# A third of the modulation's weighted sums moved from the Vector engine to GpSimd

## The reference, cut to what matters

```
def ada_modulation(cond, w, b):
    m = jax.nn.silu(cond) @ w + b
    return jnp.split(m[:, None, :], 6, axis=-1)

m_lat = ada_modulation(c, ada_w, ada_b)          # six rows of 2048
m_ctx = ada_modulation(c_ctx[None, :], ada_w, ada_b)   # rows 0 and 1 are used
hl = modulate(rmsnorm(x_lat, norm_mix), m_lat[0], m_lat[1])
x_lat = x_lat + m_lat[2] * (y_l @ w_out)
hf = modulate(rmsnorm(x_lat, norm_ffn), m_lat[3], m_lat[4])
x_lat = x_lat + m_lat[5] * peer_ffn(hf, ...)
```

## Time and profile before

| what | value |
| --- | --- |
| three runs, median | 3455.74 us (3451.08 to 3463.58) |
| profiled execution, its own time | 3448.01 us |
| its span | 3446.2 us |
| PE busy | 3109.8 us (90%) |
| DVE busy | 2464.3 us (72%) |
| ACT busy | 1886.5 us (55%) |
| POOL busy | 315.6 us (9%) |
| DVE's weighted sums, L573 | 128 instructions, 301.0 us |

### The profile page before, as it was taken

The page is one execution under the profiler, slowest core; times in us unless marked ns, Lnnn a source line. Parts: engine busy times, 40 slices in busy tenths (PEclk is TensorE's granted clock), DMA queues, the critical chain, the costliest instruction groups (busy, mean ns, idle before and its releaser), DMA issues. The chain is left out here.

```text
span 3446.2 us, 45071 instructions
## 1 busy us (share of the span) xinstructions
PE 3109.8 (90%) x12410; PEld 2161.8 (63%) x12410; DVE 2464.3 (72%) x4379; ACT 1886.5 (55%) x4137; POOL 315.6 (9%) x422
## 2 busy tenths in 40 slices
PE   5999988999999999967778489999999899999996
PEld 4887766887887878755556322222222588888885
DVE  5778766887767568753775889988888655555555
ACT  4555544555546655432344277787777555555553
POOL 0000000000000000000000033333333100000000
PEclk9999998999999999967888755555555799999998
DMA  5666664766766558930444199999999755555553
GB/s 194 211 212 220 190 200 160 256 232 228 236 219 221 173 153 275 346 141 7 154 163 167 43 374 381 366 366 386 383 383 380 269 194 187 192 195 187 191 195 122
DMA packets 213971, 788.41 MB, mean 229 GB/s; under 512 B 18515, under 2 KB 19667, under 8 KB 151251
## 3 DMA queue, kind: packets, MB, share of 16 engines
q1 hardware_dynamic: 159904, 407.33, 35.3%
q0 software_dynamic: 50688, 369.12, 28.6%
q10 hardware_dynamic: 3252, 10.41, 0.8%
HBM read 781.55 MB, written 5.24 MB: 228 GB/s over the span
## 5 line engine op out<-in xcount | busy, mean ns | idle before, releaser
L520 ACT ACTIVATE w_hi<-raw 128x512 fp32r<-128x512 f32 x880 | 545.6, 631 | 654.2 <-PE bank L535 596.4
L524 DVE TENSOR_TENSOR w_lo<-raw,w_hi 128x512 fp32r<-128x512 f32 x944 | 626.0, 693 | 350.8 <-ACT w_hi L520 333.8
L2182 DVE CUSTOM_DVE_ANT_0 u_ring<-u_ring,bank 128x1024 f32<-128x1024 f32 x512 | 604.6, 1218 | 79.1 <-DMA u_ring<-in_peer_u,idx 65.3
L533 PE MATMUL bank<-w_hi,xt_hi 128*128 128x512 f32 x1376 | 556.8, 405 | 28.5 <-DVE w_lo L524 28.3
L2249 DVE TENSOR_TENSOR w_lo<-v_raw,w_hi 128x512 fp32r<-128x512 f32 x512 | 354.4, 693 | 298.8 <-ACT w_hi L2233 298.8
L2094 PE MATMUL bank<-row_ring,three 3*128 3x512 bf16 x1024 | 517.3, 616 | 35.7 <-DVE act_in L2182 18.4
L535 PE MATMUL bank<-w_hi,xt_lo 128*128 128x512 f32 x1376 | 540.2, 393 | 0.0
L534 PE MATMUL bank<-w_lo,xt_hi 128*128 128x512 f32 x1376 | 540.1, 392 | 0.0
L2233 ACT ACTIVATE w_hi<-v_raw 128x512 fp32r<-128x512 f32 x512 | 323.8, 633 | 331.4 <-PE bank L2271 327.2
L2269 PE MATMUL bank<-w_hi,vw_hi 128*128 128x512 f32 x1024 | 404.3, 395 | 7.1 <-DVE w_lo L2249 7.1
L2271 PE MATMUL bank<-w_hi,vw_lo 128*128 128x512 f32 x1024 | 401.9, 393 | 0.0
(11 more groups left out here) (405 smaller groups left out, 3865.6 us busy)
## 6 DMA issues: line engine op xcount, KB each, us to landing
v_raw<-in_peer_v SPq DMA_DIRECT2D x128, 1024.0 KB, 4.8
ada_ring<-in_ada_w POOLq DMA_DIRECT2D x96, 1024.0 KB, 5.9
raw<-in_w_in_ab SPq DMA_DIRECT2D x128, 512.0 KB, 3.9
raw<-in_w_in_c SPq DMA_DIRECT2D x128, 512.0 KB, 4.4
raw<-in_w_in SPq DMA_DIRECT2D x120, 512.0 KB, 4.5
raw<-in_w_out_ab SPq DMA_DIRECT2D x32, 512.0 KB, 4.7
raw<-in_w_out_c SPq DMA_DIRECT2D x32, 512.0 KB, 5.7
raw<-in_w_out SPq DMA_DIRECT2D x32, 512.0 KB, 6.5
```

What stands on the lines that cost most here:

```text
L520: act.activation(w_hi[:, s % WS, :], raw[:, q % RAW, s % KC, :], ACT.Copy).then_inc(hi_ready, 1)
L524: dve.tensor_tensor(w_lo[:, s % WS, :], raw[:, s // KC % RAW, s % KC, :], w_hi[:, s % WS, :].bitcast(F32), ALU.subtract).then_inc(raw_used, 1)
L533: pe.matmul(o, a_hi, b_hi, start=kk == 0, stop=False, skip_group_check=True)
L2182: dve.tensor_tensor_reduce(u, u, bank[:, 2 * hf:2 * hf + 2, :].rearrange("p b n -> p (b n)"), 1.0, 0.0, ALU.mult, ALU.add, (act_in, act_ha ...
```

## The change

GpSimd forms the sums of the first 8 blocks of group 2, the first 8 of group 3 and all 16 of group 5. For each block it issues the load of the next one, waits for its own, multiplies the block by the factor in place (`tensor_scalar`), drains, and adds it to `acc` (`tensor_tensor`). The first block of group 3 is multiplied straight into `acc[0]`. DVE keeps the other 96 instructions. In the latent GEMM the 24 that are left there stand 13/3 steps apart, where 28 stood 11/3 apart. The memset of `acc[0]` at s == 17 of the GEMM out of c goes. The semaphore `row_summed` is replaced by a wait for `ada_used`.

```diff
+            pool.wait_ge(rows_cleared, 1)
             for k in range(K):
                 load(k, 0, k)
                 if k % 4 == 3:
                     weigh_z_pool(pool, k // 4)
-            for k in range(8):
-                load(16 + k, 2, k)
+            pool.wait_ge(bias_row_landed, 16)
+            modulations_pool(pool, load, [(16 + k, 2, k, 2) for k in range(8)])
+            pool.wait_ge(ada_used, PRE + 24)
...
-            for k in range(8):
-                load(48 + k, 3, k)
+            pool.wait_ge(acc_summed, 3)
+            modulations_pool(pool, load, [(48 + k, 3, k, 0) for k in range(8)])
             pool.wait_ge(ml_a, 2)
...
-            for k in range(K):
-                load(80 + k, 5, k)
+            pool.wait_ge(bias_row_landed, 32)
+            modulations_pool(pool, load, [(80 + k, 5, k, 3) for k in range(K)])
+
+        def modulations_pool(pool, load, steps):
+
+            load(*steps[0][:3])
+            for n, (i, g, k, to) in enumerate(steps):
+                if n + 1 < len(steps):
+                    load(*steps[n + 1][:3])
+                pool.wait_ge(ada_landed[i % 2], 16 * (i // 2 + 1))
+                pool.wait_ge(ada_used, PRE + i)
+                w, o = ada_ring[:, i % 2, :], acc[to][:, :]
+                if to < 2 and k == 0:
+                    pool.tensor_scalar(o, w, c_col[:, 0, 0:1], None, ALU.mult).then_inc(ada_used, 1)
+                else:
+                    pool.tensor_scalar(w, w, c_col[:, 0, k:k + 1], None, ALU.mult)
+                    pool.drain()
+                    pool.tensor_tensor(o, o, w, ALU.add).then_inc(ada_used, 1)
...
-            if not ab:
-                dve.drain().then_inc(row_summed, 1)
...
-                    if s == 17:
-                        dve.memset(acc[0][:, :], 0.0)
...
-                if ab and s == 6:
-                    dve.wait_ge(bias_row_landed, 16)
-                if ab and s % 8 == 7:
-                    modulate(dve, 16 + s // 8, 0, s // 8, 2)
-                if not ab and s in ADA_SLOTS_OUT:
-                    k = ADA_SLOTS_OUT.index(s)
-                    modulate(dve, 48 + k, 0, k, 0)
...
-            pe.wait_ge(row_summed, i - 1)
+            pe.wait_ge(ada_used, PRE + 48 * (i - 1))
...
-                for i in range(28):
-                    if s == 72 + i * 11 // 3:
-                        if i == 24:
-                            dve.wait_ge(bias_row_landed, 32)
-                        grp, k = (3, 8 + i) if i < 8 else (4, i - 8) if i < 24 else (5, i - 24)
-                        modulate(dve, 56 + i, 0, k, {3: 0, 4: 1, 5: 3}[grp])
+                for i in range(24):
+                    if s == 72 + i * 13 // 3:
+                        grp, k = (3, 8 + i) if i < 8 else (4, i - 8)
+                        modulate(dve, 56 + i, 0, k, {3: 0, 4: 1}[grp])
...
-                if s % 5 == 1 and s < 60:
-                    modulate(dve, 84 + s // 5, 0, 4 + s // 5, 3)
-            dve.drain().then_inc(row_summed, 1)
```

More of the change, by code:

```diff
@@ L745, in bass_hybrid_stack_kernel @@
         ADA_SLOTS_C = (4, 14, 18, 24, 28, 31, 34, 46, 49, 62)
-        ADA_SLOTS_OUT = (18, 22, 31, 38, 42, 46, 54, 58)
         ADA_SLOTS = (4, 18, 28, 31, 34, 46, 49, 62)
```

## The result

The changed kernel takes 3566.8 us, median of four runs (3553.96 to 3573.14); the kernel before 3455.97 us in the same rounds. The ratio is 1.0314, with a 95% interval of 1.028 to 1.0348: 3.1% slower. The profiled execution took 3553.96 us (span 3552.2), 106 us more than that of before. It is the fastest of the four.

The account below looks back on a forecast made before the run. PE was taken to lead in the GEMMs, with DVE slack there. 80 (GEMMs out of a layer) + 70 (group 5) - 14 (removal) = +136 us, 3584, adjusted to 3588 us; own range 3540 to 3620, 8 in 10 3480 to 3650.

Parts of the forecast that it names:

- The removal: DVE loses 32 sums; PE regains waits for w_lo, mainly in mix_out and the latent GEMM: a gain of 14 us.
- The lengths on GpSimd: Per block on GpSimd: multiplication 2.4 us, addition 4.8 us, 7.9 us in all with load issue and drain.
- GpSimd keeps DVE out: GpSimd's addition, and by assumption its multiplication, stops DVE instructions with two SBUF inputs until it ends.
- The GEMMs out of a layer: GEMMs out of ab and c, 16 blocks: each block loses 6.0 us in ab, 4.3 in c; 80 us in all.
- Group 5: 16 blocks behind the latent GEMM: 5 us for the last w_lo, 65 us in the gate rows; 70 us in all.
- The waits moved cost nothing: Added or moved waits (acc_summed, rows_cleared, sum_row_pe) cost nothing, as POOL is done with group 5 before about 1650 us.
- Strict alternation: Rival, chance 0.2: DVE gets one instruction per gap everywhere, and PE falls to the lower clock (some 10 us); 3633 us.
- Additions alone: Rival, chance 0.2: only GpSimd's additions stop DVE, its multiplications do not; +43 us, 3495 us.
- DVE's turn: Rival, chance 0.06: POOL waits where DVE runs back to back, its work stretched into DVE's idle time; 3438 us.
- the signs named: In 431 to 564 us mean w_lo over 1.5 us; PE's w_lo waits grow tens of us; gate rows 60+ us.

Follow-up runs that it names:

- experiment 1: The changed kernel without GpSimd's arithmetic: it still issues the loads and counts them as used, nobody does those 32 sums; 3427.1 us, ratio 0.9909.
- experiment 2: The changed kernel without GpSimd's multiplication, so blocks are added unscaled; 3517.6 us, ratio 1.0176.
- experiment 3: The changed kernel without GpSimd's addition, so 31 blocks are scaled in place and added nowhere; 3484.3 us, ratio 1.0081.
- experiment 4: The changed kernel with two memsets of the block in place of GpSimd's multiplication and addition (31 blocks); 3442.5 us, ratio 0.9958.
- experiment 7: The kernel without GpSimd's arithmetic, plus two group 5 blocks multiplied and added by GpSimd at gate rows and convolution; 3433.0 us in one execution.
- Experiment 8: The changed kernel with a constant (1.5) in place of the multiplication's factor read from SBUF; 3571.1 us in one execution.
- experiment 5: The kernel before with only the 16 blocks of group 5 formed on GpSimd, groups 2 and 3 staying on DVE; 3506.7 us, ratio 1.0139.

## Why the prediction was right

Forecast 3588 us (3540 to 3620), measured 3566.8: direction and cause hold, with +111 us where +132 was forecast against the median of before. Inside the terms the mechanism was partly another one, and errors cancelled. By its steps:

- *The removal, forecast -14 us.* It is worth 29 us (experiment 1). What PE waited for w_lo is no upper bound: the GEMMs out of ab and c gave 3.9 and 5.0 us instead of 2 in sum, in ab by the attention chain, where sums stood between its DVE steps. The latent GEMM gave 11.6 us, of which the summed waits for w_lo showed 7.2. Over the latent GEMM ACT's waits for weights fell from 37.2 to 18.1 us; the prediction had put such waits down as already contained.
- *The lengths on GpSimd.* The addition, forecast 4.8, is 4.6 us. The multiplication, forecast 2.4 from "half the inputs", is 5.6, outside the bound of 4.8 that I took from the addition. A block is 11.2 us, not 7.9, or 9.0 with the gaps for DVE. The error did less than its size, since the multiplication holds two-input instructions for only 3.7 of its 5.45 us, a behaviour that was not foreseen. That two errors of opposite sign met is luck.
- *GpSimd keeps DVE out.* Shown by experiments 2 to 4 and 7. The two stretched w_lo of the earlier trace rows were the whole evidence. They sufficed for the addition; that the multiplication stops DVE too was an assumption, and it came true. The rule of the Trainium skill ("SBUF — State Buffer", "SBUF: two separate sides"), that the pair is held for a whole instruction, agrees for the addition. It is too coarse for the multiplication, which let two-input instructions through 1.7 us before its end. For memsets it agrees: that section has two SBUF inputs contend only with a GpSimd instruction that reads SBUF, and in experiment 4 two-input instructions pass in 0.15 us beside a memset.
- *The GEMMs out of a layer, forecast 80 us.* Against experiment 1 they lose 43.6 and 28.9 us, 72.5 in sum. Right within 10%, and in the forecast order, ab dearer than c. But the path was wrong in ab. The forecast counted w_lo, "each w_lo lets PE do one step", and PE's waits for w_lo there are only 2.0 us; it waited 40 us in sum for the attention chain (12 before). And the forecast had nothing for the clock: 10 and 12 us of these losses are PE working at the lower level. It had named that, with some 10 us, only in its rival. So the size is partly luck. POOL began at 442, not 429, and one of its eight blocks in c is a multiplication only.
- *Group 5, forecast 70 us.* 56.5 us for gates to mix_out and 2.7 in the latent GEMM. The gate rows lose 36 instead of 65 us: a gap lets more than 1.5 instructions pass, as in the multiplication's last 1.7 us. The rest came where I had put nothing, in the mixers and the first unit, because POOL worked until 1721 us and not until about 1650. That the sum came near 70 us is luck as well.
- *The waits moved cost nothing.* `sum_row_pe` at the end found group 5 ready, as said.
- *The rivals.* Strict alternation fell with the gate rows: 30 DVE instructions in 51.9 us beside ten of POOL's arithmetic, three to one. Additions alone is refuted by experiment 3. DVE's turn did not show: POOL was idle for 15.3 us in all before its 31 additions, and its instructions kept close to their length. Of the signs named, three came: the mean of w_lo in 431 to 564 us is 1.53 us with a maximum of 5.1, the addition takes 4.6 us, and mix_out's waits fell from 7.4 to 3.4 us. Three did not: the gate rows grew to 52, not 60 or more; the multiplication takes 5.45, not 2 to 2.8 us; and PE's waits for w_lo grew by tens of us in neither GEMM (2.0 and 13.2 us).

Open: why POOL's multiplication is slower than its addition. Experiment 8 excludes the factor only. Two-input work in place of it was shorter (3.6 us and 1.1 us of idle time).

## What to carry to other kernels

An idle GpSimd is no free engine for elementwise work beside DVE: 321 us of its work that relieved DVE of 75 us cost 140 us, against 29 us that the relief was worth. Before work is moved there, look in the trace for a single instruction of it beside DVE's, and ask of each DVE instruction in reach whether it reads a PSUM bank (not held) or SBUF alone (held). Count the clock too: where PE is made to wait, it may come back to its work at the lower clock (10 and 12 us here). Look for DVE's idle stretches on the path first; spacing and moving the same sums gained 20 us without a new engine.

## What the runs showed of the hardware that was not expected

- POOL's `tensor_scalar` on 128 x 2048 f32 takes 5.45 us, with a factor from SBUF or a constant; its `tensor_tensor` takes 4.5 to 4.6 us.
- What is held depends on both instructions. Beside POOL's multiplication DVE's two-input SBUF instructions wait 3.7 us into it, and its one-input copies and `tensor_scalar` until the end. Beside a memset the one-input ones wait for its end, the two-input ones next to nothing. Beside the convolution's instructions, which read a bank and one SBUF tile, nothing is held. Small instructions are held like large ones: 4 x 2 elements took 4.1 us.
- Which record begins first does not tell who waits. Two w_lo that began 0.3 to 0.4 us before POOL's addition were held; a scan that began 0.13 us before one passed.
- POOL can pause for 6.9 us between a multiplication and an addition with DVE idle (experiment 5). Such a pause beside a busy DVE is no sign that DVE keeps it out.
